# A three-pass fp32 decoder block: a third seven-product step in each gate/up block, PSUM halves that swap from block to block, and two of three weight sums on VectorE

## The reference, cut to what matters

```python
hf = rmsnorm(x, norm_ffn[l])
act = jax.nn.silu(jnp.einsum('bsd,df->bsf', hf, w_gate[l])) * jnp.einsum('bsd,df->bsf', hf, w_up[l])
x = x + jnp.einsum('bsf,fd->bsd', act, w_down[l])
```

## Time and profile before

| | |
|---|---|
| device time, median of 3 | 1749.66 us |
| the profiled execution | 1750.99 us |
| its span, first to last instruction | 1749.2 us |
| mean granted TensorE clock | 0.997 |
| gate/up turns | 1019.27 to 1497.88 us of the span |
| TensorE busy in the span | 1732.9 us (99%) |
| VectorE, ScalarE, GpSimd busy | 992.0, 793.5, 180.7 us |

### The profile page before, as it was taken

The page is one execution under the profiler, slowest core; times in us unless marked ns, Lnnn a source line. Parts: engine busy times, 40 slices in busy tenths (PEclk is TensorE's granted clock), DMA queues, the critical chain, the costliest instruction groups (busy, mean ns, idle before and its releaser), DMA issues.

```text
span 1749.2 us, 21136 instructions
## 1 busy us (share of the span) xinstructions
PE 1732.9 (99%) x7817; PEld 1435.2 (82%) x7817; DVE 992.0 (57%) x749; ACT 793.5 (45%) x706; POOL 180.7 (10%) x109
## 2 busy tenths in 40 slices
PE   9999999999999999999999999999999999999997
PEld 7888888888888888888888878888888888888886
DVE  5454455566565544444444576777777776544445
ACT  6444344444444433333334455444444444444444
POOL 1000010100000000000000122222332321000000
PEclk9999999999999999999999999999999999999999
DMA  8656655555565555555556555555555555555552
GB/s 283 194 177 192 182 163 184 168 168 171 166 191 193 192 193 190 194 185 196 186 197 220 180 183 192 192 193 196 196 196 199 196 192 198 210 192 192 193 192 95
DMA packets 152106, 331.09 MB, mean 189 GB/s; under 512 B 8736, under 2 KB 8832, under 8 KB 146048
## 3 DMA queue, kind: packets, MB, share of 16 engines
q1 hardware_dynamic: 152064, 330.51, 56.4%
HBM read 328.38 MB, written 2.10 MB: 189 GB/s over the span
## 4 chain that ended last, share of the span: by engine, by line
PE 97%; DVE 1%; ACT 1%; POOL 1%; DMA 0%; issue 0%; SPq 0%; DVEq 0%; POOLq 0%; ACTq 0%
PE ps L1342 18%; PE ps L1343 18%; PE ps L1351 18%; PE ps L1619 9%; PE ps L1620 9%; PE ps L1624 9%; PE ps L1689 4%; PE ps L1696 4%; PE ps L1691 4%; PE ps L1360 1%; PE ps L1580 1%; DVE w_lo L882 1%; DMA xn<-in_x 0%; ACT sq_y L865 0%; ACT w_hi L497 0%
## 5 line engine op out<-in xcount | busy, mean ns | idle before, releaser
L882 DVE TENSOR_TENSOR w_lo<-w_raw,w_hi 128x2048 fp32r<-128x2048 f32 x308 | 730.5, 2374 | 505.7 <-ACT w_hi L497 503.6
L497 ACT ACTIVATE w_hi<-w_raw 128x2048 fp32r<-128x2048 f32 (+1 forms) x309 | 589.3, 1910 | 446.5 <-PE ps L1343 214.0
L1342 PE MATMUL ps<-w_hi,xT_hi 128*128 128x512 f32 x1024 | 404.6, 395 | 0.2 <-ACT w_hi L497 0.2
L1343 PE MATMUL ps<-w_hi,xT_lo 128*128 128x512 f32 x1024 | 398.7, 389 | 0.0
L1351 PE MATMUL ps<-w_lo,xT_hi 128*128 128x512 f32 x1024 | 253.0, 389 | 0.0
L1342 PEld LDWEIGHTS ps<-w_hi,xT_hi 128*128 128x128 f32 x1024 | 192.3, 188 | 40.4 <-ACT w_hi L497 0.4
L1351 PEld LDWEIGHTS ps<-w_lo,xT_hi 128*128 128x128 f32 x1024 | 192.2, 188 | 39.9
L1343 PEld LDWEIGHTS ps<-w_hi,xT_lo 128*128 128x128 f32 x1024 | 192.4, 188 | 39.0
L1619 PE MATMUL ps<-w_hi,fT_hi 128*128 128x512 f32 x440 | 173.7, 395 | 2.6 <-ACT w_hi L497 2.2
L1620 PE MATMUL ps<-w_hi,fT_lo 128*128 128x512 f32 x440 | 171.7, 390 | 0.0
L475 POOL TENSOR_TENSOR t_raw<-w_raw 128x1024 f32<-128x1024 f32 x22 | 58.6, 2665 | 801.4 <-DMA w_raw<-in_w_up 801.4
(11 more groups left out here) (220 smaller groups left out, 1733.2 us busy)
## 6 DMA issues: line engine op xcount, KB each, us to landing
w_raw<-in_w_in SPq DMA_DIRECT2D x127, 1024.0 KB, 5.5
w_raw<-in_w_gate SPq DMA_DIRECT2D x88, 512.0 KB, 3.6
w_raw<-in_w_up SPq DMA_DIRECT2D x88, 512.0 KB, 4.5
w_raw<-in_w_down SPq DMA_DIRECT2D x44, 1024.0 KB, 4.8
w_raw<-in_w_branch_a SPq DMA_DIRECT2D x16, 1024.0 KB, 4.9
w_raw<-in_w_branch_b SPq DMA_DIRECT2D x16, 1024.0 KB, 5.0
w_raw<-in_w_out SPq DMA_DIRECT2D x16, 1024.0 KB, 5.1
xn<-in_x SPq DMA_DIRECT2D x4, 512.0 KB, 8.7
```

The costliest lines, as they stand in the source:

```text
L497: copy = lambda o, i, **kw: nc.scalar.activation(o, i, ACT.Copy, **kw)
L882: V.tensor_tensor(w_lo[:, chunk.split, :], w_raw[:, chunk.raw, :], w_hi[:, chunk.split, :].bitcast(F32), ALU.subtract).then_inc(lo_split, 1)
L1342: T.matmul(ps[:, banks + r, :], rows(hi, k, r), w, start=(q == 0 and k == 0), stop=False)
L1343: last = T.matmul(ps[:, banks + r, :], rows(lo, k, r), w, start=False, stop=False)
```

## The change: what it does

It makes `STEPS` `ssSsSsSs`: steps 2, 4 and 6 are seven-product steps, 183 matmuls a turn. P1, P6 and P7 are closed after step 6. `pair_banks` gives a turn its banks: in even turns P2, Q5, Q3, Q4 are banks 4 to 7 and P1, P6, P7, FREE banks 0 to 3; in odd turns the other way round, so that a turn opens its four plain banks in those that the turn before closed first. Step 0 goes through all banks without waits in between. Loops run over two turns. GpSimd makes the sums of step 2 only; those of steps 4 and 6 are made by VectorE, at steps 2 and 4 of its program. VectorE's P6 and P7 additions come ahead of its split of the next turn's first chunk; swiglu and both silu move behind the split of the next turn's second chunk; the transposes move to steps 2 and 3. There are 22 forms for 20, 10 in the first group and 12 in the second. The start of the down part runs its first two chunks interleaved.

The diff, cut to its core:

```diff
-STEPS = "SssSssss"
-PAIR_OF = (0, 2, 3, 1, 4, 5, 6, 7)
-LAST_S = 3
-B_P1, B_P6, B_P2, B_Q3, B_Q4, B_FREE, B_P7, B_Q5 = range(8)
+STEPS = "ssSsSsSs"
+PAIR_OF = (0, 2, 3, 1, 4, 6, 5, 7)
+LAST_S = 6
+PLAIN_OF = (3, 2)
+def pair_banks(odd):
+    main, other = (0, 4) if odd else (4, 0)
+    names = ("P2", "Q5", "Q3", "Q4")
+    others = ("P1", "P6", "P7", "FREE")
+    return {n: main + k for k, n in enumerate(names)} | {n: other + k for k, n in enumerate(others)}
...
# GpSimd
-            weight_sums(0, 0)
+            first_sums(0)
             pool.wait_ge(x1_summed, 1)
             rstd_of(x1_mean, sums[:], sums[:], r_x[:, 1, :], 1, D, x1_rstd)
-            weight_sums(LAST_S, 0)
             with pool.Fori(1, FB) as i:
-                for j in (0, LAST_S):
-                    weight_sums(j, i)
+                first_sums(i)
...
# ScalarE, a turn
+                    if j == LAST_S + 1:
+                        act.wait_ge(lo_used, Chunk(G_FFN + LAST_S, i, 2 * BC).count(1))
...
+                        copy(c_gate[:, 0, :], ps[:, banks["P1"], :]).then_inc(p1_out, 1)
                     if j < 2 * BC - 1:
                         pair_split(j + 1, i)
...
                     if not first and j == 0:
+                        silu(i - 1, 0)
                         silu(i - 1, 1)
-                    if not first and j in (1, 2):
-                        act_taken(i - 1, j - 1)
+                    if not first and j in (3, 4):
+                        act_taken(i - 1, j - 3, banks["FREE"])
...
# VectorE
+            def weight_sums(j, i):
...
+                dve.wait_ge(pair_landed[c.raw], 32 * (j // RAW_SLOTS + 1) + i * 64)
+                if not (starts(i) and j == FIRST_S):
+                    dve.wait_ge(t_lo_done, before)
+                V.tensor_tensor(t_raw[:, 0:2, :], raw[:, 0:1, :].to_broadcast([P, 2, COLS]), raw[:, 1:3, :],
+                                ALU.add).then_inc(t_step, 1)
+                dve.wait_ge(t_step, before * T_STEPS + 1)
+                V.tensor_tensor(raw[:, 0, :], t_raw[:, 0, :], raw[:, 2, :], ALU.add).then_inc(t_step, 1)
+                dve.wait_ge(t_step, before * T_STEPS + 2)
+                V.tensor_tensor(t_raw[:, 2, :], raw[:, 0, :], raw[:, 3, :], ALU.add).then_inc(t_step, 1)
...
+            def ffn_turn(i, odd, last=False):
...
+                    if j == LAST_S + 1:
+                        dve.wait_ge(p1_out, i + 1)
...
+                    if j in (FIRST_S, FIRST_S + 2):
+                        weight_sums(j + 2, i)
+                    if first and j == FIRST_S:
+                        f_low(NB - 1, NB, 2, 1)
+                        forms(1, form_raw1, PLAIN_OF[1])
+                    if first and j == FIRST_S + 1:
+                        forms_low(1, form_raw1, FORM_AT[1], FORM_AT[2] - FORM_AT[1])
+                    if j < 2 * BC - 1:
+                        pair_split(j + 1, i)
...
+                    if not first and j == 0:
+                        swiglu(i - 1)
...
+                if last:
+                    stage(Chunk(G_DOWN))
+                    split(Chunk(G_DOWN))
+                add(4, c_gate[:, 1, :], "Q4", c_gate[:, 1, :], ALU.add)
...
# TensorE, a turn
+                    if not first and j == 0:
+                        pe.wait_ge(u_step, i * 2)
+                    if not first and j == FIRST_S:
+                        pe.wait_ge(c_step, i * 5 - 1)
+                    pair_step(j, i, odd)
...
+                    if not first and j in (2, 3):
+                        turn_act(i - 1, j - 2, free)
...
# TensorE, start of down
+            high(0, ALL, start=True)
+            pe.wait_ge(c_step, FB * 5 - 2)
+            high(1, (0, 1), start=True)
             pe.wait_ge(lo_split, G_DOWN + 1)
...
+            high1(0, ALL)
+            pe.wait_ge(dve_out, V_FFN + FB)
+            for h in range(2):
+                turn_half(c_up, h, LAST_TURNED + h, act_turned)
+            high1(1, (0, 1))
+            pe.wait_ge(act_out_of, 2 * FB)
+            high(1, (2, 3), start=True).then_inc(hi_used, 1)
+            low(1, (2, 3)).then_inc(lo_used, 1)
+            high1(1, (2, 3)).then_inc(hi_used, 1)
+            pe.wait_ge(lo_split, G_DOWN + 2)
+            low1(0, ALL)
+            low1(1, ALL).then_inc(lo_used, 1)
```

More of the change, by code:

```diff
@@ L844, in down_turn @@
                         split(c.next())
+                        stage(c.next())
                         if starts(i) and n == 0:
-                            silu(FB - 1, 1)
+                            for r in range(RT):
+                                silu(FB - 1, r)
                             for h in range(2):
[L848 to L854, removed]
+                                act_taken(FB - 1, h, LAST_TURNED + h)
+            ffn_turn(0, False)
+            with act.Fori(0, FB // 2 - 1) as i:
+                ffn_turn(i * 2 + 1, True)
+                ffn_turn(i * 2 + 2, False)
+            ffn_turn(FB - 2, True)
+            ffn_turn(FB - 1, False, last=True)
             down_turn(0)
@@ L1180, in forms @@
                 sums = KB - plain
+                at_s = slice(0, sums) if g else slice(plain, KB)
+                at_p = slice(sums, KB) if g else slice(0, plain)
                 s1, s2, s4 = (raw[:, KB + plain + k * sums:KB + plain + (k + 1) * sums, :] for k in range(3))
@@ L1267, in ffn_turn, with swiglu @@
+            def swiglu(i):
                 for r in range(RT):
@@ L1289, in down_turn @@
                     c = Chunk(G_DOWN + n, i, RAW_SLOTS)
-                    if last and n == RAW_SLOTS - 2:
+                    if starts(i) and n == 0:
+                        stage(c.next())
+                        swiglu(FB - 1)
+                        split(c.next())
+                    elif last and n == RAW_SLOTS - 2:
                         stage(c.next())
@@ new lines, in pair_step, with high @@
+                begins = lambda name: j == (FIRST_S if name in extra else 0)
+                own = lambda name: [p for p in parts if p[0] == name]
+                def high(part):
+                    name, tile, u = part
+                    T.matmul(ps[:, banks[name], :], tile_of(0, k, tile), moving(0, u),
+                             start=begins(name) and part is own(name)[0], stop=False)
+                    return T.matmul(ps[:, banks[name], :], tile_of(1, k, tile), moving(0, u), start=False, stop=False)
@@ L1626, in pair_step, with low @@
+                def low(part):
+                    name, tile, u = part
+                    return T.matmul(ps[:, banks[name], :], tile_of(0, k, tile), moving(1, u), start=False,
+                                    stop=final(name) and part is own(name)[-1])
                 pe.wait_ge(hi_split, c.count(1))
@@ L1628, in pair_step @@
                     pe.wait_ge(t_hi_done, S_BEFORE[j] + i * S_TURNS + 1)
-                if 0 < j < 2 * BC - 1:
-                    for part in parts:
-                        last = high(part, False)
-                    last.then_inc(hi_used, 1)
+                if j == 2 * BC - 1:
                     pe.wait_ge(lo_split, c.count(1))
-                    for n, part in enumerate(parts):
-                        last = low(part, final(part[0]) and part[0] not in [p[0] for p in parts[n + 1:]])
-                    last.then_inc(lo_used, 1)
+                    for name in dict.fromkeys(p[0] for p in parts):
+                        for part in own(name):
+                            last = high(part)
+                        if name == "Q4":
+                            last.then_inc(hi_used, 1)
+                        for part in own(name):
+                            last = low(part)
+                        last.then_inc(lo_used if name == "Q4" else bank_done, 1)
```

265 lines of the change are left out of this document (116 added, 149 removed).

## The result

| | before | changed |
|---|---|---|
| median of 5 runs each, one chip | 1749.66 us (1749.37 to 1751.49) | 1740.60 us (1740.31 to 1741.10) |
| ratio of the medians, 95% interval | | 0.9945 [0.9932, 0.9959] |
| profiled execution, its span | 1750.99, 1749.2 | 1741.1, 1738.9 |

What follows compares the result with a forecast made beforehand. Gate/up was taken as bound by TensorE's number of matmuls. 6.9 (ten turns) + 4.9 + 0.4 (turn 0) - 0.4 (down) = 11.8 us off 1750.99, 1739.2; median 1.3 lower, so 1738.0, range 1736.3 to 1743.5.

Steps and rivals of the forecast that it cites:

- Matmuls: Gate/up turns: 3 fewer matmuls in each of 11 turns, 7.5 us; a steady turn becomes 42.44 us.
- Turn 0: First gate/up turn: pause and low clock go, 42.44 us for 47.34, 4.9 us less, and 0.4 at its start.
- The chain I had: Turn 0, before step 4: VectorE's splits, sums and forms until about 1035.8, then ScalarE's form_hi, t_hi, w_hi until 1040.6.
- margin of 0.2 us: Turn 0, step 4: ScalarE's chain ends at 1040.6, TensorE wants it at 1040.8; no stall taken.
- Rival A: Turn 0 or start of down: a stall with a low clock, costing 1.9 to 4.1 us, 1740 to 1742; chance 0.20.
- the stall at the start of down: Chunk 2 of down: a new stall of about 1.5 us for 1.1 lost before, 0.4 us worse.
- Sums: Steady turns: a set on VectorE takes 2.6 us, one 1024-column instruction and two of 512; other end 6.8.
- Banks: Step 0 no longer waits for additions of the turn before; nothing on the path before, nothing gained.
- Rival B: Steady turns: sums above 3.9 us a set bring a short stall each turn; 1745 to 1750; chance 0.10.
- the blocking by GpSimd at the seam: Between turns: GpSimd's sums of step 2 slow VectorE's split, costing VectorE at most some 1.5 us a turn.
- The rule that the prediction cites: A VectorE instruction with two SBUF inputs and a GpSimd instruction reading SBUF shut each other out for one whole instruction.
- the low clock of turn 0: Kernel before, turn 0: granted clock 0.71 then 0.59 behind the 2.3 us pause, costing 1.9 us.

Runs made afterwards that it cites:

- at 5.1: Changed kernel with the first instruction of each VectorE set of sums done twice more, a set costing 5.1 us: 1745.15 us, one run.
- two swapped lines in turn 0: Kernel before, with GpSimd making turn 0's second set of weight sums ahead of the norm's root: 1747.06 us, ratio 0.9982.
- set of 6.4 us: Changed kernel with the first instruction of each VectorE set of sums done three times more: 1772.34 us, one run.

## Why the prediction was right

*Matmuls.* 42.44 us a turn, forecast and measured. With two S steps for three the kernel is 7.35 us slower, where 11 turns of three matmuls make 7.5.

*Turn 0.* Forecast 42.44, measured 466.99 - 10 x 42.44 = 42.6. The chain I had is in the trace, ScalarE in turn 0:

```profile
1036.45 1.49 ACT L506 ACTIVATE form_hi<-form_raw 128x1536 fp32r<-128x1536 f32 x1 [3.26 <-DVE form_raw L1224]
1037.85 1.47 ACT L506 ACTIVATE t_hi<-t_raw 128x1536 fp32r<-128x1536 f32 x1
1039.22 3.71 ACT L506 ACTIVATE w_hi<-w_raw 128x2048 fp32r<-128x2048 f32 x2
```

`w_hi` of step 4, the first of the two in the last row, ends at 1041.1, and step 4 is due at 1041.7. In place of a margin of 0.2 us it has 0.6, and with 1.25 us more in the sums it breaks, as shown. The margin of the forecast was no margin: its terms for VectorE add up to 12.45 us from 1023.6, so to 1036.05 and not 1035.8, and `w_hi` would then be 0.1 late. Measured, the same chain takes 12.0 us (1024.42 to 1036.42), because each instruction starts a little before the one ahead of it is shown to end. That the turn stayed clean was right, but not secured by the working. Rival A, a stall with a low clock, happened at neither place: the stall at the start of down came, and the clock stayed at 1.00 behind it.

*Sums.* 2.6 us forecast; 1.22 + 2 x 0.69 = 2.6 measured.

*Banks.* The forecast put them at nothing. That holds against the kernel before, whose waits in step 0 cost no idle time, but with this order of steps the swap is worth 1.2 us a turn. I had not worked that out.

*Rival B* gave 3.9 us as the set from which TensorE is held up. It is about 5: at 5.1 a turn is only 0.15 us longer, where B's reckoning (two pairs at 1.2 over, less 0.9 of slack) gives 1.5. So the slack that VectorE has in the rest of the turn was sized wrong: 0.9 reckoned, 2.25 by this run. VectorE's work in a turn was put at 36.6 us and is 34.3. Of the difference 1.5 is swiglu, 0.74 us an instruction for the 1.52 that the rows of before had beside GpSimd's sums. Splits follow each other after 2.21 us rather than 2.29, and the blocking by GpSimd at the seam is 0.4 us of a split for my 1.5 a turn. VectorE at the seam, then GpSimd:

```profile
1227.47 0.69 DVE L1273 TENSOR_TENSOR c_up<-ps,c_gate 128x512 f32<-128x512 f32 x1 [3.13 <-ACT c_gate L506]
...
1229.27 2.63 DVE L894 TENSOR_TENSOR w_lo<-w_raw,w_hi 128x2048 fp32r<-128x2048 f32 x1 [0.38 <-ACT w_hi L506]
1231.82 0.68 DVE L1302 TENSOR_TENSOR c_gate<-ps,c_gate 128x512 f32<-128x512 f32 x1
1232.42 0.68 DVE L1302 TENSOR_TENSOR c_up<-ps,c_up 128x512 f32<-128x512 f32 x1
```

```profile
1227.33 2.42 POOL L486 TENSOR_TENSOR t_raw<-w_raw 128x1024 f32<-128x1024 f32 x1 [35.21 <-DMA w_raw<-in_w_up]
1229.83 3.24 POOL L489 TENSOR_TENSOR w_raw<-t_raw,w_raw 128x512 f32<-128x512 f32 x1
```

GpSimd's first instruction runs mostly while VectorE waits for the P1 copy and adds P6 and P7. The second takes 3.24 us, where the third of the set, of the same size, takes 1.29 at 1233.15 with nothing to wait for; it ends 1.2 us after the split does. The split itself was held only some 0.4 us, and additions with one operand from PSUM take 0.68 beside it. The rule that the prediction cites from the Trainium skill (SBUF — State Buffer, Who interferes with whom) agrees with these rows in both directions: the one that comes second waits until the instruction ahead of it is over, and here that is mostly GpSimd. In the run with all sums on GpSimd it even waited out two splits in a row.

*Where the 2.6 us between 1738.0 and 1740.6 are.* The span is 1.5 over the forecast's 1737.4. The term sized wrong is the start of down: 13.3 forecast, 13.80 measured. Its chain begins when chunk 0 gives its `w_hi` slot free and ScalarE splits chunk 2:

```profile
1495.73 1.92 ACT L506 ACTIVATE w_hi<-w_raw 128x2048 fp32r<-128x2048 f32 x1 [1.33 <-issue]
```

That is 9.1 us after the start of down, for the 8.7 of 34 matmuls and the transposes; the rest of the chain takes 4.7 us to TensorE's start at 1500.46, as forecast. Turn 0 is 0.2 of the 1.5. The other 0.8 is the start: turn 0 began at 1019.67, for 1018.9. Repeated, the changed kernel began it at 1018.73 with a span of 1737.9, and over ten profiles of variants that leave this part alone it lies between 1018.3 and 1019.7. So it is scatter of the first 25 us; what makes it the runs don't show. The rest is between span and time: the profiled execution of before took 1.8 us over its span and was 1.3 above the median, which I took off; that of the change 2.2 and 0.5. If the low clock of turn 0 is in some executions only, as the times above suggest, then the forecast was also wrong to take off the 1.3 and to count the low clock in full.

## What to carry to other kernels

List for each repeated piece when it is ready and when it is due. The sum of an engine's work says little until it is near the whole turn (40.3 of 42.6 us was still nearly free in the steady turns), and an idle engine is no use if the chain through it is too long (GpSimd, busy for 25 of 46 us). A pause can cost the low clock as well, in the trace of before 1.9 us on top of 2.3, so look at such pauses first: two swapped lines in turn 0 were worth 3.1 us, two fifths of what the 33 matmuls brought, and needed nothing of this change. Where an engine makes something small that the next stage waits for, put it ahead of its long instruction.

## What the runs showed of the hardware

The clock behind a pause does not go by its length alone. A pause of 2.16 us in the kernel before brought 0.59. The one of 2.38 us with all sums on VectorE, shown above, left it at 1.00. Here are one of 2.78 us in turn 0 (set of 6.4 us), with the stretch behind it, and one of 2.87 us (all sums on GpSimd), with the two stretches behind it:

```profile
1055.21 1.20 PE L1682 MATMUL ps<-w_lo,fT_hi 128*128 128x512 f32 x4 [2.78 <-DVE w_lo L895]
...
1058.00:1060.00 2.00, 2.00 (x6) 1.59 (x5) 2.00 (x2) 0.07 (x1) 0.00 (x0) 0.50 0.78 301
```

```profile
1056.13 0.50 PE L1673 MATMUL ps<-w_hi,fT_hi 128*128 128x512 f32 x1 [2.87 <-ACT w_hi L510]
...
1057.00:1058.50 1.50, 1.50 (x8) 1.25 (x7) 1.50 (x2) 0.89 (x1) 0.00 (x0) 1.00 0.00 0
1058.50:1060.00 1.50, 1.50 (x8) 1.23 (x7) 1.50 (x1) 0.00 (x0) 0.00 (x0) 1.00 0.26 44
```

After the first the clock stands at 0.50, the lower level of 1.2 GHz; after the second, longer one it stays at 1.00, 2.4 GHz. What makes the difference the runs don't show.
